# Second mixer's attention by pairs of heads, rotated parts of two heads from the two halves of the rows, first output tiles among the last heads

## What is computed

```python
def block_softmax_attention(q, k, v):          # q: 256 x 8 x 192, k: 512 x 8 x 192, v: 512 x 8 x 128
    scale = Dh ** -0.5
    def one(qblk):                              # blocks of 128 queries
        s = jnp.einsum('bqhd,bkhd->bhqk', qblk, k).astype(jnp.float32) * scale
        p = jax.nn.softmax(s, axis=-1).astype(v.dtype)
        return jnp.einsum('bhqk,bkhv->bqhv', p, v)
...
    o = block_softmax_attention(q, jnp.concatenate([kc, k], axis=1), jnp.concatenate([vc, v], axis=1))
    out = o.reshape(B, L, MLA_HEADS * MLA_V) @ w_out
```

## Time and profile before

| | us |
|---|---|
| median of 3 runs (1394.15 to 1402.97) | 1398.13 |
| the profiled execution, its own time | 1395.81 |
| its span | 1394.0 |
| PE busy | 1352.2 (97%) |
| ACT busy | 676.8 (49%) |
| DVE busy | 582.3 (42%) |
| POOL busy | 708.6 (51%) |

### The profile page before, as it was taken

How to read it: one execution, slowest core, us unless ns; L and a number is a source line. 1 busy time by engine, 2 the same in 40 slices (tenths; PEclk the granted TensorE clock), 3 DMA queues, 4 the chain that set the end, 5 groups by cost and what they waited for, 6 DMA issues and landing times.

```text
span 1394.0 us, 22410 instructions
## 1 busy us (share of the span) xinstructions
PE 1352.2 (97%) x8316; PEld 1122.0 (80%) x8316; DVE 582.3 (42%) x1076; ACT 676.8 (49%) x1036; POOL 708.6 (51%) x307
## 2 busy tenths in 40 slices
PE   4999999999999999999999999999999998999998
PEld 1578787777888888877768755999999986999998
DVE  4413475324543344300025654455532475455510
ACT  1553134433544444422136843576665667666642
POOL 0433002253444444434444510588899774698896
PEclk9999999999999999999999999999999999999999
DMA  9323644353233332346673310466667541465663
GB/s 359 149 76 91 226 153 151 138 209 136 91 105 92 92 103 90 105 152 212 211 266 110 102 30 1 161 200 195 193 200 211 180 136 46 166 192 191 191 211 106
DMA packets 60069, 210.19 MB, mean 151 GB/s; under 512 B 6368, under 2 KB 9696, under 8 KB 59872
## 3 DMA queue, kind: packets, MB, share of 16 engines
q1 hardware_dynamic: 59568, 207.52, 45.4%
q10 hardware_dynamic: 432, 1.70, 0.3%
HBM read 208.15 MB, written 1.05 MB: 150 GB/s over the span
## 4 chain that ended last, share of the span: by engine, by line
PE 90%; DVE 3%; DMA 2%; ACT 2%; issue 2%; SPq 1%; ACTq 0%; DVEq 0%
PE ps L309 70%; PE ps L399 2%; DMA raw<-wstream 2%; PE ps L921 2%; PE ps L1233 1%; PE ps L354 1%; PE ps L1232 1%; PE ps L915 1%; PE ps L907 1%; PE ps L1242 1%; PE ps L355 1%; PE ps L346 1%; SPq L285 1%; PE ps L848 1%; DVE ps L574 1%
## 5 line engine op out<-in xcount | busy, mean ns | idle before, releaser
L298 POOL TENSOR_TENSOR wlo<-raw,whi 128x1024 fp32r<-128x1024 f32 x291 | 696.3, 2410 | 662.8 <-ACT whi L293 662.2
L293 ACT ACTIVATE whi<-raw 128x1024 fp32r<-128x1024 f32 x291 | 306.4, 1055 | 244.4 <-DMA raw<-wstream 138.3
L309 PE MATMUL ps<-Hhi_,whi 128*128 128x256 f32 (+1 forms) x1352 | 393.6, 319 | 0.0
L309 PE MATMUL ps<-Hlo_,whi 128*128 128x256 f32 (+1 forms) x1352 | 389.0, 316 | 0.0
L309 PEld LDWEIGHTS ps<-Hhi_,whi 128*128 128x128 f32 x1352 | 253.9, 188 | 26.7 <-issue 5.4
L309 PEld LDWEIGHTS ps<-Hlo_,whi 128*128 128x128 f32 x1352 | 253.9, 188 | 20.1 <-issue 1.9
L309 PE MATMUL ps<-Hhi_,wlo 128*128 128x256 f32 (+1 forms) x1352 | 234.3, 316 | 0.0
L309 PEld LDWEIGHTS ps<-Hhi_,wlo 128*128 128x128 f32 x1352 | 196.6, 188 | 18.4
L309 PE MATMUL ps<-hidhi,whi 128*128 128x256 f32 (+1 forms) x528 | 151.8, 316 | 0.0
L309 PE MATMUL ps<-hidlo,whi 128*128 128x256 f32 (+1 forms) x528 | 150.8, 314 | 0.0
L635 ACT ACTIVATE u<-ps,par 128x256 f32<-128x256 f32 (+1 forms) x132 | 83.8, 635 | 120.4 <-PE ps L309 114.3
(11 more groups left out here) (302 smaller groups left out, 1646.9 us busy)
## 6 DMA issues: line engine op xcount, KB each, us to landing
raw<-wstream SPq DMA_DIRECT2D x387, 512.0 KB, 3.8
XT<-x_t SPq DMA_DIRECT2D x1, 1024.0 KB, 11.7
XT<-ctx_t SPq DMA_DIRECT2D x1, 1024.0 KB, 13.9
memx<-mem_t ACTq DMA_DIRECT2D x1, 1024.0 KB, 5.6
out_t<-XT SPq DMA_DIRECT2D x1, 1024.0 KB, 5.1
par<-params SPq DMA_DIRECT2D x1, 457.5 KB, 3.4
glac<-gla_consts SPq DMA_DIRECT2D x1, 384.0 KB, 9.0
mlac<-mla_consts ACTq DMA_DIRECT2D x1, 320.0 KB, 7.3
```

Of the source, the lines that this page charges most:

```text
L293: nc.scalar.activation(whi[:, n % RING, :], raw[:, r % RAWS, :], ACT.Copy).then_inc(S["hi_ready"], 1)
L298: nc.gpsimd.tensor_tensor(wlo[:, r, :], raw[:, r, :], whi[:, n % RING, :].bitcast(F32), ALU.subtract).then_inc(S["lo_ready"], 1)
L309: mm = nc.tensor.matmul(o, a, b, start=start, stop=stop)
```

## The change

Heads go in pairs p = (2p, 2p+1), and the unit of work is a pair and a query block `qt`, with its two heads in two neighbouring banks.

- Scores: two plain matmuls (128 rows), then two rotated ones (64 rows), one from each half of the rows, one signal for all four. PE's order: scores(0,0), scores(0,1), then for each pair turns(p,0), scores(p+1,0), turns(p,1), scores(p+1,1), outputs(2p), outputs(2p+1).
- Maxima: one reduction over both banks (128x1024) in place of two. There is one reciprocal (128x2) for each `qt` of a pair, eight in all as before; the number of exponentials, scalings, transposes, copies and head outputs stays.
- Both heads' transposes of one `qt` use banks 4 and 5; `PTm` gets a second buffer, one for each head of the pair.
- Key norms 2 and 3 come after the first and second reduction.
- Output tile 0 gets its products with heads 0 to 5 ahead of outputs(6), tile 1 its own after outputs(7); then heads 6 and 7 for both. Tiles 2 to 7 are column tiles as before.

```diff
-            PTm = sb(part, "PTm", [P, 4, T])
+            PTm = sb(part, "PTm", [P, 2, 4, T])
...
-            def scores(h):
...
-                    nc.tensor.matmul(ps[:, bank, :], mq[:, h, qs], kn[:, h, :], start=True, stop=False)
-                    nc.tensor.matmul(ps[:, bank, :], mq[r0:r0 + 64, 8 + h // 2, qs], kpe[r0:r0 + 64, :],
-                                     start=False, stop=True).then_inc(S["a_s"], 1)
+            def scores(p, qt):
+
+                qs = slice(qt * P, (qt + 1) * P)
+                pe.wait_ge(S["m_qn"], p + 1)
+                pe.wait_ge(S["m_kn"], p + 1)
+                if p >= 1:
+                    pe.wait_ge(S["a_exp"], 4 * (p - 1) + 2 * qt + 2)
+                for e in range(2):
+                    nc.tensor.matmul(ps[:, 2 * qt + e, :], mq[:, 2 * p + e, qs], kn[:, 2 * p + e, :], start=True, stop=False)
+                for e in range(2):
+                    r = slice(64 * e, 64 * e + 64)
+                    mm = nc.tensor.matmul(ps[:, 2 * qt + e, :], mq[r, 8 + p, qs], kpe[r, :], start=False, stop=True)
+                mm.then_inc(S["a_s"], 1)
+
+            def turns(p, qt):
+
+                for e in range(2):
+                    pe.wait_ge(S["a_pn"], 4 * p + 2 * qt + e + 1)
+                    if p >= 1 or qt == 1:
+                        pe.wait_ge(S["a_pt"], 4 * p + 2 * qt + e - 1)
+                    for kt in range(4):
+                        mm = nc.tensor.transpose(ps[:, 4 + e, kt * P:(kt + 1) * P], Pm[:, e, qt, kt * P:(kt + 1) * P], ident)
+                mm.then_inc(S["a_t"], 1)
...
             def outputs(h):
-                pe.wait_ge(S["a_pt"], 2 * h + 2)
+                pe.wait_ge(S["a_pt"], 4 * (h // 2) + 3 + h % 2)
...
+            def out_part(tile, h0, h1):
...
+                for h in range(h0, h1):
+                    pe.wait_ge(S["a_oh"], 2 * (h + 1))
+                    o, n, c = ps[:, tile, 0:T], (mo + tile) % RING, slice(h * P, (h + 1) * P)
+                    nc.tensor.matmul(o, whi[:, n, c], Nhi[:, h, 0:T], start=h == 0, stop=False)
+                    nc.tensor.matmul(o, whi[:, n, c], Nlo[:, h, 0:T], start=False, stop=False)
+                    mm = nc.tensor.matmul(o, wlo[:, RAW_OF[mo + tile] % RAWS, c], Nhi[:, h, 0:T], start=False, stop=h == MH - 1)
...
+            scores(0, 0)
+            scores(0, 1)
+            for p in range(MH // 2):
                 for qt in range(2):
...
+                    turns(p, qt)
+                    if p + 1 < MH // 2:
+                        scores(p + 1, qt)
+                if p == MH // 2 - 1:
+                    pe.wait_ge(S["a_exp"], 16)
+                    out_part(0, 0, 6)
+                outputs(2 * p)
+                outputs(2 * p + 1)
+            out_part(1, 0, 6)
+            out_part(0, 6, MH)
+            out_part(1, 6, MH)
+            for m in range(2, KD):
+                pe.wait_ge(S["mo_x"], m + 1)
+                column_tile(pe, mo + m, m % 4, *N(0, T), T)
...
+            def exps(p, qt):
+                for e in range(2):
+                    act.wait_ge(S["a_max"], 2 * p + qt + 1)
+                    if p >= 1:
+                        act.wait_ge(S["a_t"], 2 * (p - 1) + qt + 1)
...
+            def turned(p, qt):
+                act.wait_ge(S["a_t"], 2 * p + qt + 1)
+                if p >= 1:
+                    act.wait_ge(S["a_o"], 2 * p)
+                for e in range(2):
+                    nc.scalar.activation(PTm[:, e, :, qt * P:(qt + 1) * P], ps[:, 4 + e, :].rearrange("p (k q) -> p k q", q=P),
+                                         ACT.Copy).then_inc(S["a_pt"], 1)
+            act.wait_ge(S["m_kn"], 2)
+            exps(0, 0)
+            exps(0, 1)
+            act.wait_ge(S["m_kn"], 4)
+            for p in range(MH // 2):
                 for qt in range(2):
...
+                    turned(p, qt)
+                    if p + 1 < MH // 2:
+                        exps(p + 1, qt)
...
+            key_norm(0)
+            key_norm(1)
...
+                nc.vector.tensor_reduce(amx[:, qt, :], ps[:, 2 * qt:2 * qt + 2, :], AX_X, ALU.max, negate=True).then_inc(S["a_max"], 1)
...
+            maxes(0, 0)
+            key_norm(2)
+            maxes(0, 1)
+            rows(0, 0)
+            key_norm(3)
+            rows(0, 1)
+            for p in range(1, MH // 2):
+                maxes(p, 0)
+                rows(p, 0)
+                maxes(p, 1)
+                split_out(2 * p - 2)
+                rows(p, 1)
+                split_out(2 * p - 1)
             split_out(MH - 2)
             split_out(MH - 1)
```

More of the change, by code:

```diff
@@ L1241, in outputs @@
                 for kt in range(4):
-                    mm = nc.tensor.matmul(ps[:, 6 + h % 2, 0:T], mv[:, kt, h * P:(h + 1) * P], PTm[:, kt, :], start=kt == 0, stop=kt == 3)
+                    mm = nc.tensor.matmul(ps[:, 6 + h % 2, 0:T], mv[:, kt, h * P:(h + 1) * P], PTm[:, h % 2, kt, :], start=kt == 0, stop=kt == 3)
                 mm.then_inc(S["a_o"], 1)
[L1245 to L1249, removed]
-                for qt in range(2):
[L1251 to L1258, removed]
@@ L1259, in mla_pe @@
-            outputs(MH - 1)
-            out_pe(pe, "mo", lambda k: Nhi[:, k, 0:T], lambda k: Nlo[:, k, 0:T], T, S["mo_x"], S["a_oh"], 2)
+            mo = START["mo"]
+            def out_part(tile, h0, h1):
+                pe.wait_ge(S["hi_ready"], mo + tile + 1)
+                pe.wait_ge(S["lo_ready"], mo + tile + 1)
+                for h in range(h0, h1):
[4 more added lines that the diff above has]
+                    mm = nc.tensor.matmul(o, wlo[:, RAW_OF[mo + tile] % RAWS, c], Nhi[:, h, 0:T], start=False, stop=h == MH - 1)
+                    if h == MH - 1:
+                        mm.then_inc(S["slot_used"], 1)
@@ new lines, in mla_pe @@
+            keep_running(pe, 7, 12)
+            pe.wait_ge(S["m_rot"], 2)
+            pe.wait_ge(S["m_ev"], 14)
+            scores(0, 0)
+            scores(0, 1)
+            for p in range(MH // 2):
+                for qt in range(2):
+                    turns(p, qt)
[6 more added lines that the diff above has]
+                outputs(2 * p + 1)
@@ L1313, in mla_act @@
                         inverse_root(Hf1[:, 2 * i:2 * i + 2, :]).then_inc(S["m_krstd"], 1)
-            def exps(h):
-                for qt in range(2):
[L1317 to L1334, removed]
+            def exps(p, qt):
[3 more added lines that the diff above has]
+                        act.wait_ge(S["a_t"], 2 * (p - 1) + qt + 1)
+                    nc.scalar.activation(Pm[:, e, qt, :], ps[:, 2 * qt + e, :], ACT.Exp, bias=amx[:, qt, e:e + 1],
+                                         accum_out=asum[:, qt, e:e + 1]).then_inc(S["a_exp"], 1)
+            def turned(p, qt):
[10 more added lines that the diff above has]
+            for p in range(MH // 2):
+                for qt in range(2):
+                    turned(p, qt)
+                    if p + 1 < MH // 2:
+                        exps(p + 1, qt)
             out_act(act, "mo", T, S["mo_x"])
@@ L1392, in mla_dve, with maxes, rows @@
             nc.vector.tensor_tensor(kpe[:, T:TT], kpe[:, T:TT], mrst[:, 0, 0:T], ALU.add).then_inc(S["m_rot"], 1)
[L1394 to L1400, removed]
+            key_norm(0)
+            key_norm(1)
+            def maxes(p, qt):
+                dve.wait_ge(S["a_s"], 2 * p + qt + 1)
+                if p >= 1:
+                    dve.wait_ge(S["a_exp"], 4 * (p - 1) + 2 * qt + 2)
+                nc.vector.tensor_reduce(amx[:, qt, :], ps[:, 2 * qt:2 * qt + 2, :], AX_X, ALU.max, negate=True).then_inc(S["a_max"], 1)
+            def rows(p, qt):
+                dve.wait_ge(S["a_exp"], 4 * p + 2 * qt + 2)
+                if p >= 1:
+                    dve.wait_ge(S["a_pn"], 4 * (p - 1) + 2 * qt + 2)
+                dlink(nc.vector.reciprocal(arec[:, qt, :], asum[:, qt, :]))
+                for e in range(2):
+                    x = Pm[:, e, qt, :]
+                    nc.vector.tensor_scalar(x, x, arec[:, qt, e:e + 1], None, ALU.mult).then_inc(S["a_pn"], 1)
             def split_out(h):
```

12 lines of the change are left out of this document (removed).

## The result

The changed kernel takes 1386.94 us (median of 5 runs, 1384.73 to 1393.3); the kernel before, run beside it, 1398.13 (5 runs, 1394.15 to 1402.97). The ratio is 0.9927, 95% interval 0.9901 to 0.9954 (it isn't the quotient of the two medians, which is 0.9920). Forecast were 1388.1 and a range of 1381 to 1396. The profiled execution took 1393.3, more than the other four (1384.7 to 1388.5), so its span can't be read as the kernel's gain.

What follows compares the result with a forecast made beforehand. PE was taken to bound the attention up to its tail; 10.1 us less PE work on scores, minus 0.2 balance of waits, gave about 10 us, so 1398.1 - 10.0 = 1388.1, range 1381 to 1396.

Steps and rivals of the forecast that it cites:

- The halves overlap: Scores: two rotated parts in opposite row halves run together, 0.86 us instead of 1.72; rival without overlap 1395.0, chance 0.06.
- Period of a pair 11.1: Steady part of the attention: a pair of heads takes 11.1 us instead of 13.5.
- Chain through DVE and ACT: Steady part: slack 0.5 us, new waits priced at nothing; rival that the chain binds: 3.5 won, 1394.6, chance 0.07.
- Waits: PE: new waits of 2.2 us at the start and 0.9 in the tail; 2.9 of old tail waits go.
- Tile products among the heads as mere cover: Tail: moving output tile products wins nothing itself, only covers copies and split; without cover the wait would be 1.2 us.
- What is late next: Behind the attention: tiles 0 and 1 end about 869, tile 4 is ready with slack 1.6 us, everything later just shifts.
- full clock throughout: Sign expected in the profile after: the granted clock stays full, with no lower level behind the first wait.
- its chance for 8 to 12 us won: Whole kernel: the forecast case, 8 to 12 us won, a single short clock stretch included, chance 0.74.
- the rival's "Against": Clock rival, first wait: lower clock loses 1.7 us per stretch, slower kernel chance 0.03; against it, PE's unbroken work around the wait.

Runs made afterwards that it cites:

- doubled reduction: Every reduction of two banks made twice, one behind the other, against the changed kernel; 1397.48 us (11 runs), ratio 0.998 to the kernel before.
- filled variant: Changed kernel with four idle products in PE's first wait, between scores(0,1) and turns(0,0); 1386.42 us (6 runs), ratio 0.9928 to the kernel before.

## Why the prediction was right, and where it was not

- The time: 1388.1 forecast, 1386.94 and 1387.63 measured. That they lie within 1.2 us is in part luck: the differences to before are 11.2 in one set and 8.7 in the other. In the stage 10 us were forecast; the trace shows 10.4 at full clock and 8.7 with the low clock.
- The halves overlap: right. A rotated pair was taken at 0.86 plus a change of shape; it has 1.06 in all. Undone alone it costs 6.7 (forecast 6.9); undone with the changes of shape 9.9 (forecast 10.1). The lower figure worked out from the Trainium skill ("TensorE: Matmul & The Clock Gate", section on packing small matmuls) was a rotated pair of 1.12; this trace doesn't agree, with 0.86. The page has four tiles of 32 rows, here are two of 64.
- Period of a pair 11.1: right, 11.11.
- Chain through DVE and ACT: right. The reduction over two banks has 1.23 (taken: 1.22), PE never waits in the steady part, and the doubled reduction shows the slack as 0.5, the value worked out.
- Waits: 2.2 at the start against 1.92; 0.9 in the tail against 0.78; none of 1.24, as forecast. Both are a little shorter than worked out, which is most of the 0.4 between 10.0 and 10.4.
- Tile products among the heads as mere cover, 1.2 if it were gone: 1.05.
- What is late next: nothing; no wait of PE for weights follows. Tile 1 is done at 870.82, not near 869, by the 1.7 of low clock; in the filled variant it is done at 869.44, from a start 0.5 later.
- Wrong: "full clock throughout". The prediction named a clock that falls behind the first wait as a sign that it is wrong, and that sign came; its chance for 8 to 12 us won, on the other hand, included one such stretch. The step that failed is the rival's "Against", that PE working without a break before and after the wait would keep the clock, as it did behind the 1.24 of the earlier trace rows. A wait of 1.9 to 3.8 us was followed by the lower level in 7 of 8 profiles (3.4 us of it in five, 6.8 in two), and in the attention one of 0.62 or 1.24 in none (two profiles each). The size was right (1.7 for one stretch, as the rival had it from the earlier trace rows), its place wasn't: it belonged into the sum. With it the forecast would have been 1389.8, still inside its range; the shorter waits point the other way by 0.4, and the rest of the distance to 1386.94 is less than the scatter of the runs.
- The length of a wait alone doesn't decide, though. The third block, the same in all versions, has a wait of 1.24, and in 4 of the 13 profiles the lower level stands behind it. One is the second profile of the kernel before, timeline and window:

```profile
1158.71 1.81 PE L1562 MATMUL ps<-cacc,con 128*128 128x256 f32 x4 [1.24 <-DVE cacc L1760]
```

```profile
1159.02:1162.43 3.41, 3.41 (x14) 2.69 (x14) 1.71 (x4) 2.69 (x10) 1.46 (x2) 0.50 0.00 0
```

- The wait of 1.87 of the earlier trace rows is followed by it in 12 of 13. And the profile with the filled wait has such a stretch (234.13 to 237.54, granted 0.50) at a wait of 0.35, far ahead of the attention. So the rival's "Against" was weak on the kernel before already, but only its second profile shows that, and that one was taken after the prediction.
- Not seen at all: the two paces. What they do to the medians can't be told, but the profiled execution of after had the slower one for 168 us, and who reads its span alone finds 2.5 us won and looks for a loss of 6 in the change.

## What to carry to other kernels

Two matmuls with 64 rows each cost as much as one here if they stand behind each other, in opposite halves of the rows and in different banks; each switch between shapes costs 0.2 here, so group by shape. When a change takes away the work that covered the first pass through another engine, price the wait that appears and also a stretch of low clock behind it: here 1.9 us of standing cost 1.7 more, and moving one reduction behind the first scaling took 1.3 us off the wait and removed the low clock in both profiles of that order. Judge a stage by its own stretch of the trace and not by the span, when the same kernel's spans differ by 7.7 us outside it.

## What the hardware showed that was not expected

- The lower clock level follows a single wait of 1.9 us between two dense stretches (granted 0.50 or 0.51), for 3.4 us or for 6.8, but not each time: one profile of eight had the wait and kept 1.00. In the third block it follows a wait of 1.24 us in 4 profiles of 13 and one of 1.87 in 12.
- Two rotated matmuls of 64 rows in opposite halves start within 0.01 us of each other and take 0.86 together, what one takes alone; in the same half they take 1.91 with the change of shape, against 1.06.
- The 256-column products of the split float32 operands have two paces at a granted clock of 1.00, 113 and 118 ns from start to start (records of 276 and 281 ns). A pace lasts for most of a stage or more (867 to 1035 in the first profile of the changed kernel), and it differs between executions of one kernel. Which one is taken at a restart, and why the output tiles of this stage were slower in nine profiles of the changed order and quicker in both of before, no run here settles.
